# One row gather of a mixture-of-experts stage: 32 leftover rows packed, high part and low part, into one zero-padded block of 128

## The chip, the cores and the metric

The kernel runs on one core of one Trainium2 chip. The metric is the device time of one execution in microseconds (us). The kernel before was timed three times: the median is 1857.46 us, the lowest 1855.92 us and the highest 1864.35 us. A separate execution was profiled; the trace and every row below come from that one.

The core has five engines that run side by side and meet only at semaphores: TensorE (PE in the profile; its weight loads are shown apart, as PEld), VectorE (DVE), ScalarE (ACT), GpSimd (POOL) and SyncE (SP), which here only issues loads and stores.

## The reference

The reference is one inference step of a two-layer decoder over 256 prompt rows and 32 sample rows (8 sequences of 4) of width 1024. Layer 0 is block-sparse attention and a dense feed-forward; layer 1 is dilated window attention and a mixture of 8 experts, of which each row takes 2. Only the last part is touched by the change:

```
logits = x @ w_router                       # (288, 8)
top_val, top_idx = top_k(logits, 2)
gates = softmax(top_val)
# every expert e takes the rows that chose it, in blocks of 128 slots:
out[block] = swiglu(x_pad[toks], w_gu[e], w_down[e])
y[row] = sum over its two experts of gate * out[its slot]
```

All of it is float32.

## The kernel before

**Precision by parts.** TensorE gets 32-bit operands rounded to a shorter format ("fp32r"). To keep float32 accuracy every matrix is cut into a high part (the rounded value) and a low part (what the rounding left), and a product is three matmuls: high·high, high·low and low·high. The function `three` does this for the weights (lines 241, 242 and 243, the lines that fill the profile).

**Weights.** Weights arrive in pieces of 128 x 2048 floats (1 MB). SP loads them into a ring of six buffers `raw`; ACT makes the high part `whi` (L233), DVE the low part `wlo` (L237), each into a ring of three; PE uses a piece in 12 matmuls. ACT may start on piece p when PE is done with piece p-3 (semaphore `pieces_used`), SP may load piece p when DVE is done with piece p-6 (`pieces_split`). An expert has 42 pieces: 28 of gate and up weights, then 14 of down weights.

**Rows.** The 288 normalized rows lie in SBUF as three blocks (`TB`): 128, 128 and 32 rows, one row in a partition, 1024 columns. `hth` holds their high part, `htl` their low part. An expert's block of 128 slots is gathered by matmuls: `pm` is a one-hot matrix (row of the block by slot), written by DVE from a row's slot number (`one_hot`), and pm · rows, summed over the three blocks and both parts, gives the gathered rows in PSUM, in two halves of 512 columns (`gather`, L735). So a gather is 2 halves x 2 parts x 3 blocks = 12 matmuls; the third block is a matmul with 32 rows of weights. ACT copies each half to `xgs` (L1013), PE turns it in eight transposes (`gather_turn`, L745), ACT and DVE cut the result into `xgh` and `xgl`.

**Order in an expert.** The order on each engine is written out by hand, in the functions `expert(n)`. On PE the gate and up matmuls go in seven groups of four pieces. Between them stand: the transposes of the activations (`turn`, L755), the scatter of the expert before (`scatter`, L719: six matmuls twice), after piece 15 the turn of the one-hot matrix (`one_hot_turn`, L726: three transposes, released by DVE's last `add_rows`), and after piece 21 the gather for the next expert. DVE builds the next one-hot after piece 20's low part (L1426, at step 18 of its loop). Eight experts ran in this execution, so there are nine gathers, one ahead of the loop and eight in it, and eight one-hot turns.

**Ahead of the loop.** DVE, ACT and POOL make the rows: DVE copies them from PSUM (L1360), ACT squares them for the norm (L999), DVE scales (L1365), ACT makes `hth` (L1005), POOL makes `htl` (L400), DVE works out the routing in a long chain of small operations (L1383 to L1419), clears `pmt` (L1453), and writes the first one-hot. Then comes the first gather, and after it a second chain of small operations on DVE (L1465 to L1486) that stands ahead of the third piece's low part.

Of the kernel before, what the change touches and what calls it, by code (L numbers as in the profile page):

```python
# [22 lines left out]
F32 = mybir.dt.float32  # L23
F32R = mybir.dt.float32r
I32 = mybir.dt.int32
ALU = mybir.AluOpType
# [4 lines left out]
P = 128  # L31
D = 1024
# [3 lines left out]
NSAMP = NSEQ * QLEN  # L36
# [14 lines left out]
TB = [(0, P), (P, P), (2 * P, NSAMP)]  # L51
# [23 lines left out]
def build_program(nc, io):  # L75
    ctx = ExitStack()
    with ctx:
# [5 lines left out]
        def sem(name):  # L83
            if name not in named:
                named[name] = ctx.enter_context(nc.semaphore(name))
            return named[name]
# [11 lines left out]
        def at(name, off, shape, dt=F32):  # L98
            size = 4
            for s in shape[1:]:  # L100
                size *= s
            assert off + size <= REGION, name
            return nc.alloc_sbuf_tensor_at(name, shape, dt, offset=base + off)

        def con(name, rows=P):
            a, b = CONST[name]
            return cst[0:rows, a:b]
# [55 lines left out]

        xtok = at("xtok", 0, [P, 3, D])
        hth = at("hth", 12288, [P, 3, D], F32R)
        htl = at("htl", 24576, [P, 3, D], F32R)
        htok = at("htok", 36864, [P, 3, D])
        acth = at("acth", 36864, [P, KE, P], F32R)
        actl = at("actl", 51200, [P, KE, P], F32R)
# [6 lines left out]
        pm = at("pm", 86016, [P, 3, P], F32R)  # L176
# [8 lines left out]
        pcur = at("pcur", 95168, [P, 3])  # L185
# [9 lines left out]
        ps = [psum[:, i, :] for i in range(8)]  # L195
# [136 lines left out]
        @block.gpsimd  # L332
        def _(eng):
            eng.dma_start(pgt[0:1, :], io["page_table"]).then_inc(sem("pages_loaded"), 16)
            eng.wait_ge(sem("pages_loaded"), 16)

            def store(b, key, val):

                eng.wait_ge(sem(f"ktok_done_{b['tag']}"), b["nj"])
                eng.wait_ge(sem(f"vtok_done_{b['tag']}"), b["nj"])  # L340
                for buf, out in ((b["ktok"], key), (b["vtok"], val)):
                    eng.dma_start(out[0:SEQ, :].rearrange("(b p) n -> p b n", p=P), buf[:, 0:2, :]).then_inc(sem(f"kv_stored_{b['tag']}"), 16)
                    eng.dma_start(out[SEQ:T, :], buf[0:NSAMP, 2, :]).then_inc(sem(f"kv_stored_{b['tag']}"), 16)

            def caches(b, q, kt, vt):
                if q < NSEQ:
                    if q >= b["nk"]:

                        eng.wait_ge(sem(f"ktr_done_{b['tag']}"), (q - b["nk"] + 1) * b["kr"])
                    kt(q)  # L350

                if q >= 3:

                    eng.wait_ge(sem(f"spv_done_{b['tag']}"), q - 2)
                if q >= 1:
                    vt(q - 1)

            def paged(src, buf, q, done):
                for j in range(2):
                    pg = eng.value_load(pgt[0:1, 2 * q + j:2 * q + j + 1], min_val=0, max_val=NPHYS - 1)  # L360
                    eng.dma_start(buf[:, j, :], src[0][bass.ds(pg, 1), :, :].rearrange("a p n -> p (a n)")).then_inc(done, 16)

            def keys_a(q):
                paged(io["cache_a_k"], A["kraw"][:, 0], q, sem("kraw_loaded_a0"))

            def vals_a(q):
                if q == 0:

                    eng.wait_ge(sem("kv_stored_a"), 64)
                paged(io["cache_a_v"], A["vraw"][:, q % 2], q, sem(f"vraw_loaded_a{q % 2}"))  # L370

            caches(A, 0, keys_a, vals_a)
            store(A, io["ak"], io["av"])
            for q in range(1, NSEQ + 1):
                caches(A, q, keys_a, vals_a)

            def window(src, buf, q, done):
                eng.dma_start(buf, src[q].rearrange("(j p) n -> p j n", p=P)).then_inc(done, 16)

            def keys_b(q):  # L380
                window(io["cache_b_k"], B["kraw"][:, q % 2], q, sem(f"kraw_loaded_b{q % 2}"))

            def vals_b(q):
                window(io["cache_b_v"], B["vraw"][:, q % 2], q, sem(f"vraw_loaded_b{q % 2}"))


            eng.wait_ge(sem("added_dn"), KD)
            eng.dma_start(B["mask"][:, :], io["mask_b"]).then_inc(sem("mask_loaded_b"), 16)
            eng.wait_ge(sem("ktok_done_b"), B["nj"])
            eng.wait_ge(sem("vtok_done_b"), B["nj"])  # L390
            caches(B, 0, keys_b, vals_b)
            store(B, io["bk"], io["bv"])
            for q in range(1, NSEQ + 1):
                caches(B, q, keys_b, vals_b)
            eng.wait_ge(sem("o_split_b"), 1)
            eng.dma_start(rw[:, :, :], io["w_router"][0].rearrange("(k p) e -> p k e", p=P)).then_inc(sem("router_loaded"), 16)
            eng.dma_start(grow[:, :], io["g_rows"]).then_inc(sem("router_loaded"), 16)
            for c, (t0, w) in enumerate(TB):
                eng.wait_ge(sem("rows_hi"), c + 1)
                nc.gpsimd.tensor_tensor(htl[0:w, c, :], htok[0:w, c, :], hth[0:w, c, :].bitcast(F32), ALU.subtract).then_inc(sem("rows_lo"), 1)  # L400
            for b in "ab":
                eng.wait_ge(sem(f"kv_stored_{b}"), 64)

# [2 lines left out]
        def _(eng):  # L406
# [231 lines left out]
            for i in range(GU_P // 2):  # L638
                for part in range(2):
# [4 lines left out]
                    for s in range(2):  # L644
                        bank = ps[4 * (i % 2) + 2 * part + s]
                        for k in range(KD):
                            if i == 0 and part == 0 and s == 0:
                                eng.wait_ge(sem("norm_lo_ready"), norm_count("norm_f", k))
                            c = (k * 2 + s) * P
                            ins = three(bank[:, 0:T], whi[:, pc % SPL, c:c + P], wlo[:, pc % SPL, c:c + P], hh[:, k], hl[:, k],  # L650
                                        k == 0, k == KD - 1)
                        ins.then_inc(tile_sem(tiles_gu, 4 * i + 2 * part + s), 1)
            for m in range(KD + 2):
                if m < KD:
                    for part in range(2):
# [8 lines left out]
                        for k in range(11):  # L664
                            kk = 11 * part + k
                            if m == 0:
                                eng.wait_ge(sem("act_lo"), kk + 1)
                            ins = three(ps[m % 4][:, 0:T], whi[:, pc % SPL, k * P:(k + 1) * P], wlo[:, pc % SPL, k * P:(k + 1) * P],
                                        gh[:, kk], gl[:, kk], kk == 0, kk == KF - 1)
# [11 lines left out]
            for c, (t0, w) in enumerate(TB):  # L681
                for half in range(2):
                    if n == 0:
                        eng.wait_ge(sem("added_wob"), KD)
                    for u in range(4):
                        ins = nc.tensor.transpose(ps[n][0:w, u * P:(u + 1) * P], xT[:, 4 * half + u, t0:t0 + w], con("ident"))
# [4 lines left out]
            for c, (t0, w) in enumerate(TB):  # L691
                for k in range(KD):
                    ins = nc.tensor.matmul(ps[6][0:w, 8 * c:8 * c + 8], xT[:, k, t0:t0 + w], rwg[:, k], start=k == 0, stop=k == KD - 1)
# [8 lines left out]
            for d in range(3):  # L702
                wd = TB[d][1]
                ins = nc.tensor.matmul(ps[7][:, 32:40], con("ones", wd), sel[0:wd, 0, 8 * d:8 * d + 8], start=d == 0, stop=d == 2)
# [18 lines left out]
            def one_hot_turn(n):  # L723
                eng.wait_ge(sem("y_added"), 6 * n + 6)
                for c, (t0, w) in enumerate(TB):
                    ins = nc.tensor.transpose(ps[7][:, c * P:c * P + w], pm[0:w, c, :].bitcast(F32), con("ident", w)[:, 0:w])  # L726
                ins.then_inc(sem("one_hot_turned"), 1)

            def gather(n):

                eng.wait_ge(sem("one_hot"), n + 1)
                for half in range(2):
                    for part, v in enumerate((hth, htl)):
                        for c, (t0, w) in enumerate(TB):
                            ins = nc.tensor.matmul(ps[5 + half][:, :], pm[0:w, c, :], v[0:w, c, 512 * half:512 * half + 512],  # L735
                                                   start=part == 0 and c == 0, stop=part == 1 and c == 2)
                    ins.then_inc(sem("rows_gathered"), 1)

            def gather_turn(n):
# [336 lines left out]
        def _(eng):  # L1076
# [12 lines left out]
            def chain(ins):  # L1089

                steps[0] += 1
                ins.then_inc(sem("vector_step"), 1)
                eng.wait_ge(sem("vector_step"), steps[0])

            V = nc.vector
# [255 lines left out]
            for k in range(KD):  # L1351
                ins = V.tensor_scalar(rwg[:, k], rw[:, k], cst[:, g1 + k:g1 + k + 1], None, ALU.mult)
            ins.then_inc(sem("router_scaled"), 1)
            chain(V.memset(mst[:, :, :], 1.0))
            V.memset(sel[:, :, :], 0.0).then_inc(sem("mst_ready"), 1)
            n = 0
            for c, (t0, w) in enumerate(TB):
# [63 lines left out]
            def one_hot(n):  # L1421

                V.tensor_copy(pcur[:, :], pslot[:, :, bass.ds(n, 1)].rearrange("p c o -> p (c o)")).then_inc(sem("places_copied"), 1)
                eng.wait_ge(sem("places_copied"), n + 1)
                for c, (t0, w) in enumerate(TB):
                    ins = V.tensor_scalar(pm[0:w, c, :], con("slots", w), pcur[0:w, c:c + 1], None, ALU.is_equal)  # L1426
                ins.then_inc(sem("one_hot"), 1)

            def gather_lo(n, half):
                eng.wait_ge(sem("gathered_hi"), 2 * n + half + 1)  # L1430
# [18 lines left out]
                    .then_inc(sem("y_added"), 1)  # L1449


            V.memset(gcur[:, :], 0.0).then_inc(sem("gates_copied"), 1)
            V.memset(pmt[:, :, :].bitcast(F32), 0.0).then_inc(sem("pmt_copied"), 1)  # L1453
            one_hot(0)
# [199 lines left out]
```

## Time and profile before

| | before |
|---|---|
| median of 3 runs | 1857.46 us |
| profiled execution, its own time | 1856.88 us |
| its span, first to last instruction | 1855.2 us |
| mean granted TensorE clock | 0.956 |
| PE / PEld / DVE / ACT / POOL busy | 95 / 78 / 73 / 56 / 2 % of the span |

The profiled execution's own time is 1.7 us above its span and 0.6 us under the median of the runs. In a row of the timeline the columns are: start in us, duration in us, engine, line, operation, out<-in with partitions x elements, count; in brackets the idle time of that engine before it and what ended it. Matmuls overlap, since one starts before the one before it has left the array; what a matmul costs is therefore read from the distance of two starts, or from the chain of waits, where a piece is charged only for the time that it adds. A granted clock of 1.00 is 2.4 GHz and one of 0.50 is 1.2 GHz.

### The profile page before, as it was taken

To read this page: it belongs to the slowest core of one execution; us is meant where nothing else is said; L and a number is where in the kernel's file an instruction comes from. 1 tells how busy PE (TensorE), PEld (TensorE's weight loads), DVE (VectorE), ACT (ScalarE), POOL (GpSimd) and SP (SyncE) were. 2 spreads that over 40 slices of the span, in tenths; PEclk is the share of its full clock that TensorE was granted. 3 is DMA by queue.
4 is the path that set the end of the run, shared out by engine and by line. 5 is a ranking of instruction groups with operands and counts; after the bars stand their busy time and mean duration, and the time that the engine had idled before them with its cause. 6 is when DMAs were issued, how large, how long until landed. Compare 5 with 4: busy or idle time off the path is not lost.

```text
span 1855.2 us, 24910 instructions
## 1 busy us (share of the span) xinstructions
PE 1770.2 (95%) x9114; PEld 1444.4 (78%) x9114; DVE 1357.5 (73%) x1721; ACT 1038.6 (56%) x1043; POOL 44.7 (2%) x67
## 2 busy tenths in 40 slices
PE   7998989999989898689999999999999999999998
PEld 5786779999977667567887887887877878878776
DVE  5764316665557676678888888897897888888987
ACT  4333324443343243256776776766776767767765
POOL 0002100000000110100000000000000000000000
PEclk9998869999999987679999999999999999999999
DMA  9335413543653331059898998998998998999985
GB/s 319 99 114 188 149 56 114 171 155 111 185 170 107 118 117 48 13 202 343 319 362 317 359 345 315 360 344 327 354 336 330 352 346 318 362 317 359 343 319 205
DMA packets 232981, 453.17 MB, mean 244 GB/s; under 512 B 7584, under 2 KB 79264, under 8 KB 232784
## 3 DMA queue, kind: packets, MB, share of 16 engines
q1 hardware_dynamic: 224656, 422.13, 65.1%
q0 software_dynamic: 8256, 30.12, 4.9%
q8 instruction: 43, 0.70, 0.1%
q14 instruction: 26, 0.21, 0.0%
HBM read 447.50 MB, written 4.72 MB: 244 GB/s over the span
## 4 chain that ended last, share of the span: by engine, by line
PE 90%; DVE 5%; ACT 2%; issue 1%; DMA 1%; POOLq 0%; DVEq 0%; SPq 0%; ACTq 0%
PE psum L241 24%; PE psum L243 24%; PE psum L242 24%; PE psum L578 2%; PE psum L517 2%; PE psum L735 2%; PE psum L719 1%; PE psum L755 1%; PE psum L534 1%; PE psum L464 1%; PE psum L456 1%; PE psum L448 1%; PE psum L559 1%; DVE wlo L237 1%; PE psum L480 1%
## 5 line engine op out<-in xcount | busy, mean ns | idle before, releaser
L237 DVE TENSOR_TENSOR wlo<-raw,whi 128x2048 fp32r<-128x2048 f32 (+1 forms) x404 | 911.5, 2261 | 233.6 <-ACT whi L233 233.5
L233 ACT ACTIVATE whi<-raw 128x2048 fp32r<-128x2048 f32 (+1 forms) x404 | 764.8, 1895 | 326.8 <-PE psum L243 326.7
L241 PE MATMUL psum<-whi,xgh 128*128 128x512 f32 x896 | 360.5, 402 | 7.8 <-DVE wlo L237 6.4
L243 PE MATMUL psum<-whi,xgl 128*128 128x512 f32 x896 | 356.2, 398 | 0.0
L242 PE MATMUL psum<-wlo,xgh 128*128 128x512 f32 x896 | 354.4, 396 | 0.0
L241 PE MATMUL psum<-hh,whi 128*128 128x288 f32 x800 | 246.1, 308 | 11.6 <-DVE hl L1276 9.1
L243 PE MATMUL psum<-hh,wlo 128*128 128x288 f32 x800 | 239.9, 300 | 0.0
L242 PE MATMUL psum<-hl,whi 128*128 128x288 f32 x800 | 239.1, 299 | 0.0
L241 PEld LDWEIGHTS psum<-whi,xgh 128*128 128x128 f32 x896 | 169.3, 189 | 48.9 <-DVE wlo L237 6.9
L243 PEld LDWEIGHTS psum<-whi,xgl 128*128 128x128 f32 x896 | 169.2, 189 | 41.5
L242 PEld LDWEIGHTS psum<-wlo,xgh 128*128 128x128 f32 x896 | 169.4, 189 | 39.5
L241 PE MATMUL psum<-whi,acth 128*128 128x512 f32 x448 | 177.9, 397 | 0.0
L242 PE MATMUL psum<-wlo,acth 128*128 128x512 f32 x448 | 177.5, 396 | 0.0
L243 PE MATMUL psum<-whi,actl 128*128 128x512 f32 x448 | 176.9, 395 | 0.0
L241 PEld LDWEIGHTS psum<-hh,whi 128*128 128x128 f32 x800 | 153.1, 191 | 25.8 <-issue 12.2
L242 PEld LDWEIGHTS psum<-hl,whi 128*128 128x128 f32 x800 | 153.4, 192 | 0.8
L243 PEld LDWEIGHTS psum<-hh,wlo 128*128 128x128 f32 x800 | 152.7, 191 | 0.0
L241 PEld LDWEIGHTS psum<-whi,acth 128*128 128x128 f32 x448 | 84.1, 188 | 20.2
L243 PEld LDWEIGHTS psum<-whi,actl 128*128 128x128 f32 x448 | 84.1, 188 | 20.1
L242 PEld LDWEIGHTS psum<-wlo,acth 128*128 128x128 f32 x448 | 84.2, 188 | 19.6
L1043 ACT ACTIVATE sg<-psum 128x512 f32<-128x512 f32 x56 | 33.6, 600 | 46.1 <-PE psum L243 46.0
L241 PE MATMUL psum<-gh,whi 128*128 128x288 f32 x176 | 53.2, 302 | 1.2 <-issue 1.2
(290 smaller groups left out, 1805.4 us busy)
## 6 DMA issues: line engine op xcount, KB each, us to landing
raw<-in_w_gu_moe SPq DMA_DIRECT2D x226, 1024.0 KB, 5.4
raw<-in_w_down_moe SPq DMA_DIRECT2D x112, 1024.0 KB, 5.3
raw<-in_w_gu_dense SPq DMA_DIRECT2D x22, 1024.0 KB, 5.0
raw<-in_w_qkv_a SPq DMA_DIRECT2D x12, 1024.0 KB, 12.3
raw<-in_w_down_dense SPq DMA_DIRECT2D x16, 704.0 KB, 4.6
kraw_a<-in_cache_a_k POOLq DMA_DIRECT2D x16, 512.0 KB, 4.8
vraw_a<-in_cache_a_v POOLq DMA_DIRECT2D x16, 512.0 KB, 4.9
raw<-in_w_q_b SPq DMA_DIRECT2D x6, 1024.0 KB, 5.0
```

The lines of the kernel that those rows point to most:

```text
L233: nc.scalar.activation(whi[:, p % SPL, 0:size], raw[:, p % RAW, 0:size], ACT.Copy).then_inc(hi_ready, 1)
L237: nc.vector.tensor_tensor(wlo[:, p % SPL, 0:size], raw[:, p % RAW, 0:size], whi[:, p % SPL, 0:size].bitcast(F32), ALU.subtract).then_inc(p ...
L241: nc.tensor.matmul(out, lh, rh, start=start, stop=False)
L242: nc.tensor.matmul(out, lh, rl, start=False, stop=False)
L243: return nc.tensor.matmul(out, ll, rh, start=False, stop=stop)
L448: nc.tensor.matmul(ps[4 + r // 4 % 2][0:8, 0:T], cst[:, c:c + 8], sq[:, r % 2], start=r % 4 == 0, stop=r % 4 == 3)\
L456: nc.tensor.matmul(ps[6][:, 0:T], con("rot"), sq[:, 2 + r % 2], start=True, stop=True)\
L464: nc.tensor.matmul(ps[7][:, 0:T], cst[0:8, c:c + P], rs[0:8, 1], start=True, stop=True)\
L517: ins = nc.tensor.matmul(ps[SS_BANK][0:rows, 0:T], b["qblk"][:, u % 2, j * rows:(j + 1) * rows], b["keys"][:, j, :], start=j == 0, stop=j ...
L578: ins = nc.tensor.matmul(out, b["vraw"][:, u % 2, c, j * P:(j + 1) * P], b["spt"][:, u % 2, c, 8 * j:8 * j + 8], start=c == 0, stop=c == 1)
L735: ins = nc.tensor.matmul(ps[5 + half][:, :], pm[0:w, c, :], v[0:w, c, 512 * half:512 * half + 512], start=part == 0 and c == 0, stop=part ...
L1043: nc.scalar.activation(sg[:, :], ps[0][:, :], ACT.Silu).then_inc(sem("silu_done"), 1)
```

## The change

The 32 rows of the third block get their high and their low part into one block of 128 partitions: partitions 0 to 31 of `hth[:, 2, :]` hold the high part as before, 32 to 63 the low part, 64 to 127 zeros. The one-hot matrix of the third block holds the same 32 rows twice, in partitions 0 to 31 and 32 to 63, and zeros below. One matmul over all 128 partitions then adds high and low part of the 32 rows. A half of a gather takes five matmuls of full 128 rows of weights in place of six, of which two had 32. The turn of the one-hot matrix works on three full blocks. Two clears of padding are added on DVE (64 x 1024 and 64 x 128), a fourth small one-hot operation in every `one_hot`, and a wait on POOL ahead of its third subtraction.

```diff
-        htl = at("htl", 24576, [P, 3, D], F32R)
+        htl = at("htl", 24576, [P, 2, D], F32R)
...
             for c, (t0, w) in enumerate(TB):
                 eng.wait_ge(sem("rows_hi"), c + 1)
-                nc.gpsimd.tensor_tensor(htl[0:w, c, :], htok[0:w, c, :], hth[0:w, c, :].bitcast(F32), ALU.subtract).then_inc(sem("rows_lo"), 1)
+                if c == 2:
+                    eng.wait_ge(sem("rows_lo"), 2)
+                low = htl[:, c, :] if c < 2 else hth[NSAMP:2 * NSAMP, 2, :]
+                nc.gpsimd.tensor_tensor(low, htok[0:w, c, :], hth[0:w, c, :].bitcast(F32), ALU.subtract).then_inc(sem("rows_lo"), 1)
...
                 for c, (t0, w) in enumerate(TB):
-                    ins = nc.tensor.transpose(ps[7][:, c * P:c * P + w], pm[0:w, c, :].bitcast(F32), con("ident", w)[:, 0:w])
+                    ins = nc.tensor.transpose(ps[7][:, c * P:(c + 1) * P], pm[:, c, :].bitcast(F32), con("ident"))
...
                 for half in range(2):
-                    for part, v in enumerate((hth, htl)):
-                        for c, (t0, w) in enumerate(TB):
-                            ins = nc.tensor.matmul(ps[5 + half][:, :], pm[0:w, c, :], v[0:w, c, 512 * half:512 * half + 512],
-                                                   start=part == 0 and c == 0, stop=part == 1 and c == 2)
+                    for i, (v, c) in enumerate(((hth, 0), (hth, 1), (htl, 0), (htl, 1), (hth, 2))):
+                        ins = nc.tensor.matmul(ps[5 + half][:, :], pm[:, c, :], v[:, c, 512 * half:512 * half + 512],
+                                               start=i == 0, stop=i == 4)
                     ins.then_inc(sem("rows_gathered"), 1)
...
             chain(V.memset(mst[:, :, :], 1.0))
+            V.memset(hth[64:P, 2, :].bitcast(F32), 0.0)
             V.memset(sel[:, :, :], 0.0).then_inc(sem("mst_ready"), 1)
...
                 for c, (t0, w) in enumerate(TB):
-                    ins = V.tensor_scalar(pm[0:w, c, :], con("slots", w), pcur[0:w, c:c + 1], None, ALU.is_equal)
-                ins.then_inc(sem("one_hot"), 1)
+                    V.tensor_scalar(pm[0:w, c, :], con("slots", w), pcur[0:w, c:c + 1], None, ALU.is_equal)
+                V.tensor_scalar(pm[NSAMP:2 * NSAMP, 2, :], con("slots", NSAMP), pcur[0:NSAMP, 2:3], None, ALU.is_equal).then_inc(sem("one_hot"), 1)
...
+            V.memset(pm[64:P, 2, :].bitcast(F32), 0.0)
             V.memset(gcur[:, :], 0.0).then_inc(sem("gates_copied"), 1)
```

On PE, at the gather inside an expert, the program stood like this before (`am` is the activations being turned, `pm` the one-hot, `xgh` and `xgl` the gathered rows of the current expert; lines are those of the kernel before):

```order
L243 MATMUL psum<-whi,xgl 128x512
L755 MATMUL psum<-cst,am 128x128 x4
L731 REGISTER_ALU
L735 MATMUL psum<-hth,pm 128x512 x3
L735 MATMUL psum<-htl,pm 128x512 x3
L735 MATMUL psum<-hth,pm 128x512 x3
L735 MATMUL psum<-htl,pm 128x512 x3
L410 REGISTER_ALU
L241 MATMUL psum<-whi,xgh 128x512
```

and stands like this now (the last of the first half and the first two of the second are printed together as three):

```order
L757 MATMUL psum<-cst,am 128x128 x4
L734 REGISTER_ALU
L737 MATMUL psum<-hth,pm 128x512 x2
L737 MATMUL psum<-htl,pm 128x512 x2
L737 MATMUL psum<-hth,pm 128x512 x3
L737 MATMUL psum<-htl,pm 128x512 x2
L737 MATMUL psum<-hth,pm 128x512
```

Twelve matmuls became ten; what stands around them did not move.

On DVE, between the routing and the first gather, the program stood like this before (`pslot` and `gslot` are the slots and gates of all rows, `pmt` is the turned one-hot, `pcur` the slots of the expert at hand):

```order
L1418 COPY pslot<-sel 128x3x8 [waits vector_step]
L1419 COPY gslot<-sel 128x3x8 [waits vector_step]
L1452 MEMSET gcur 128x3 [waits vector_step]
L1453 MEMSET pmt 128x384
L1423 COPY pcur<-pslot 128x3
L1426 TENSOR_SCALAR pm<-cst,pcur 128x128 [waits places_copied]
L1426 TENSOR_SCALAR pm<-cst,pcur 128x128
L1426 TENSOR_SCALAR pm<-cst,pcur 32x128
L237 TENSOR_TENSOR wlo<-raw,whi 128x2048 [waits hi_ready] x2
```

and stands like this now:

```order
L1422 COPY gslot<-sel 128x3x8 [waits vector_step]
L1455 MEMSET pm 64x128 [waits vector_step]
L1456 MEMSET gcur 128x3
L1457 MEMSET pmt 128x384
L1426 COPY pcur<-pslot 128x3
L1429 TENSOR_SCALAR pm<-cst,pcur 128x128 [waits places_copied]
L1429 TENSOR_SCALAR pm<-cst,pcur 128x128
L1429 TENSOR_SCALAR pm<-cst,pcur 32x128
L1430 TENSOR_SCALAR pm<-cst,pcur 32x128
L237 TENSOR_TENSOR wlo<-raw,whi 128x2048 [waits hi_ready] x2
```

One clear and one small operation more stand ahead of the first gather; the operation of L1430 is there in every expert too, ahead of a `wlo`.

## Rows read from the trace of the kernel before

**Rows 1.** The page: the busy time of each engine, and the chain that ended last.
```profile
PE 1770.2 (95%) x9114; PEld 1444.4 (78%) x9114; DVE 1357.5 (73%) x1721; ACT 1038.6 (56%) x1043; POOL 44.7 (2%) x67
PE 90%; DVE 5%; ACT 2%; issue 1%; DMA 1%; POOLq 0%; DVEq 0%; SPq 0%; ACTq 0%
```

**Rows 2.** Windows, gather to gather: length, busy us by engine, clock, DMA share, GB/s.
```profile
874.26:1003.74 129.48, 129.48 (x569) 102.61 (x568) 110.28 (x72) 93.03 (x66) 0.00 (x0) 1.00 0.95 341
1651.14:1780.62 129.48, 129.48 (x569) 102.61 (x568) 110.29 (x72) 93.00 (x66) 0.00 (x0) 1.00 0.96 341
```

**Rows 3.** Waits, 811 to 1845 us: engine line <- releaser: us, times, longest.
```profile
ACT whi L233 <- PE psum L243: 253.6, 257, 8.0
DVE wlo L237 <- ACT whi L233: 153.5, 199, 4.2
```

**Rows 4.** Timeline around the gather in the loop's first expert.
```profile
873.66 0.60 PE L755 MATMUL psum<-cst,am 128*128 128x128 f32 x4
874.02 1.13 PE L735 MATMUL psum<-hth,pm 128*128 128x512 f32 x3
874.66 0.18 PEld L735 LDWEIGHTS psum<-hth,pm 32*128 32x128 f32 x1 [0.36 <-issue]
875.08 0.30 PEld L735 LDWEIGHTS psum<-htl,pm 128*128 128x128 f32 x2 [0.24 <-issue]
...
878.33 0.50 PE L241 MATMUL psum<-whi,xgh 128*128 128x512 f32 x1
878.67 0.40 PE L242 MATMUL psum<-wlo,xgh 128*128 128x512 f32 x1
```

**Rows 5.** Chain of waits in the loop: start, us added, what.
```profile
818.08 1.39 PE psum L719 x6
...
874.26 4.14 PE psum L735 x12
```

**Rows 6.** Timeline: an activation turn at 849 us, then the one-hot turn at 855 us.
```profile
849.58 0.60 PE L755 MATMUL psum<-cst,am 128*128 128x128 f32 x4
850.26 0.40 PE L242 MATMUL psum<-wlo,xgh 128*128 128x512 f32 x1
...
854.99 0.73 DVE L1448 SCALAR_TENSOR_TENSOR xtok<-psum,gcur,xtok 32x512 f32<-32x512 f32 x1
855.78 0.61 PE L726 MATMUL psum<-cst,pm 128*128 128x128 f32 x3
856.15 0.13 PEld L726 LDWEIGHTS psum<-cst,pm 32*128 32x128 f32 x1 [0.17 <-issue]
856.66 0.39 PE L242 MATMUL psum<-wlo,xgh 128*128 128x512 f32 x1
```

**Rows 7.** Timeline of the first gather, ahead of the loop, and two matmuls behind it.
```profile
785.08 1.91 PE L735 MATMUL psum<-hth,pm 128*128 128x512 f32 x3 [3.04 <-DVE pm L1426]
792.54 1.97 PE L745 MATMUL psum<-cst,xgs 128*128 128x128 f32 x8
798.65 0.63 PE L241 MATMUL psum<-whi,xgh 128*128 128x512 f32 x1
799.07 0.63 PE L242 MATMUL psum<-wlo,xgh 128*128 128x512 f32 x1
810.41 0.79 PE L241 MATMUL psum<-whi,xgh 128*128 128x512 f32 x1 [6.42 <-DVE wlo L237]
```

**Rows 8.** Chain of waits from 754 to 800 us, ahead of the first gather.
```profile
758.40 0.30 DVE sel L1355
758.70 3.53 DVE xtok L1360 x6
...
783.83 0.38 DVE pmt L1453
784.26 0.68 DVE pm L1426 x3
```

**Rows 9.** Timeline from 767 to 776 us: POOL's three subtractions, DVE's routing beside them.
```profile
767.78 8.01 POOL L400 TENSOR_TENSOR htl<-htok,hth 128x1024 fp32r<-128x1024 f32 x3 [24.82 <-ACT hth L1005]
773.57 2.27 DVE L1387 TENSOR_TENSOR sel<-sel,cst 128x24 f32<-128x24 f32 x1
```

**Rows 10.** Line 226, the loads, from 820 to 1840 us: issue to landing.
```profile
DMA to landing us min/median/max: 4.7/5.4/8.6
```

## The prediction, made before the changed kernel ran

> **What bounds the kernel now.** I read the page first. TensorE is busy 95% of the span and holds 90% of the chain that ended last [rows 1]. A share of busy time is a mean over stages, so I next cut the expert loop into windows from one gather to the next. Every expert takes 129.48 us, and PE is busy in all of it, at the full clock, with DVE at 110 us and ACT at 93 us [rows 2]. The list of waits says who runs behind whom: ACT waited 257 times for PE and DVE 199 times for ACT [rows 3], and PE waited for a `wlo` only once, at 810.41 us where the loop starts [rows 7]. So inside the loop time follows PE's issue of matmuls one for one, and ACT and DVE follow PE. Then I looked at the timeline of the two places that the change touches on PE, and at the chain of waits ahead of the loop, where DVE and not PE sets the pace.
>
> **The gather in the loop.** Three matmuls starting at 874.02 us are followed by the next three, whose weights load at 875.08 us: 1.06 us for three [rows 4]. A plain stream goes much faster: six L719 matmuls of the same shape and weights add 1.39 us, 0.232 us each [rows 5], so three should take 0.70. The difference sits at the matmul with 32 rows of weights. Its load begins after PEld stood idle for 0.36 us, and the load of the full block behind it after 0.24 us more [rows 4]. In a plain stream loads are pulled ahead under the running matmul. I read this as an array that must empty when the number of weight rows changes, on the way in and on the way out. The whole gather adds 4.14 us [rows 5]. The way out is also paid by the L241 matmul behind it: it starts at 878.33 and its successor at 878.67, 0.34 us instead of 0.23 [rows 4]. From the first gather matmul to that L242 it is 878.67 - 874.02 = 4.65 us.
>
> After the change these are ten full matmuls and the one L241, all with 128 rows of weights: 11 x 0.232 = 2.55 us. Saved: 4.65 - 2.55 = 2.10 us per gather. Of these, two matmuls fewer are 0.46 us, and the switching that goes is the other 1.64. Eight gathers lie in the loop: 16.8 us. Bounds: a full gather matmul can hardly beat 0.232. From above, the nearest row is the mean of today's gather, 4.14 / 12 = 0.345; with that, ten cost 3.45, the L241 keeps its 0.34, and a gather saves 4.65 - 3.79 = 0.86 us, 6.9 in all. I take 0.232, because L719 is the same shape with the same kind of operands.
>
> A rule of the Trainium skill speaks against this size: "TensorE: Matmul & The Clock Gate", section "Why this matters for your kernels", says that a lone matmul with 32 weight rows takes as long as one with 128. By that only the two dropped matmuls would count. The page "TensorEngine Tiling (Array Packing)", section "Key Properties", says that a change of tiling mode drains the engine. The spacing in the timeline goes with the second.
>
> **The one-hot turn.** The three transposes start at 855.78 us, directly behind DVE's last add (854.99 + 0.73 = 855.72), and the second matmul behind them starts at 856.66: 0.88 us. Here too the 32-row load stands idle before it, 0.17 us. The activation turn of four full transposes goes from 849.58 to the second matmul behind it at 850.26 in 0.68 us [rows 6]. One transpose less is 0.09 us (four take 874.02 - 873.66 = 0.36 in rows 4), so three full ones should take 0.59. Saved 0.29 us, times 8: 2.3 us. The release by DVE stays. If the switch cost stayed and the third transpose, now 128 wide instead of 32, cost a further 0.09, the turns would lose 0.7 us in all. I take the gain.
>
> **The first gather.** It runs at the half clock. It starts at 785.08 us and the transposes behind it at 792.54: 7.46 us [rows 7]. Matmuls at this clock start 0.42 to 0.43 us apart (798.65, 799.07), so ten take 4.27. Saved: 3.19 us. It is on the path: `xgl` follows it, then DVE's chain of small operations, then the `wlo` for which PE waits 6.42 us, to 810.41 [rows 7]. Everything in this line moves up with the gather. Should the denser stream bring the full clock sooner, PE would still wait for DVE at 810 us; only the piece between gather and `xgl` could gain, under 2 us.
>
> **What is added.** (1) The clear of 64 x 1024 of `hth` stands on DVE between two clears and the copies L1360. Clears cost about 1 ns per element of a partition: `sel`, 288 elements, 0.30 us, and `pmt`, 384, 0.38 us [rows 8]. So 1024 cost 1.05 us. The chain of waits runs through `sel` straight into the six copies, and through ACT and DVE to the first gather, so I charge all of it: 1.05 us. Between nothing (if something else hid it) and 1.1. (2) The clear of 64 x 128 of `pm`: 0.13 us, on the same path. (3) The fourth one-hot operation: 0.68 / 3 = 0.22 us [rows 8], on the path once, ahead of the first gather. In the loop it comes ahead of a `wlo` on DVE, which waits for ACT 199 times [rows 3]. DVE's 110.3 us become 110.5 of then 127.1: hidden. If that cover were gone it would cost 8 x 0.22 = 1.8 us. (4) POOL's third subtraction waits for its own two before it. POOL works until 767.78 + 8.01 = 775.79 and DVE's small operations crawl beside it, the one at 773.57 taking 2.27 us and ending at 775.84, with POOL [rows 9]. POOL is thus on the path here. The wait opens a gap of a tenth or two, in which DVE also gets an operation in; writing 32 partitions lower should not change POOL's time. I take 0, and bound it by one such operation, 2.3 us, either way. Added in all: 1.40 us.
>
> **Who could be late next.** ACT and DVE now lose 2.1 us of waiting per expert; DVE has 129.48 - 110.28 = 19.2 us of it. The loads: 341 GB/s over an expert of 129.48 us become 341 x 129.48 / 127.1 = 347. A load lands 4.7 to 8.6 us after its issue [rows 10]. Between the end of piece p-6's `wlo` and the start of piece p's `whi` lie about six pieces of 12 x 0.232 = 2.8 us, less some 4 us for splitting: 12 us. The margin over 8.6 is larger than the 2.1 us that the gather stops giving.
>
> **The sum.** 16.8 + 2.3 + 3.2 - 1.4 = 20.9 us. The profiled execution took 1856.88 us (span 1855.2), which gives 1836.0. The median of the runs lies 0.6 above that execution, so 1836.6; I say 1836.5, or 1.1% faster.
>
> **Rivals.**
> A. The empty time does not come from the 32 rows but from alternating operands, and each gather matmul keeps its 0.345 us. Then the loop gathers save 8 x 2 x 0.345 = 5.5 us, the turns nothing, the first gather 2 x 7.46 / 12 = 1.2 less the added 1.4: 5.3 in all, 1852. For it: no row of before shows a gather without 32-row blocks. Against it: the idle stands exactly at the 32-row load and at the one behind it, and L719 alternates between `oh` and `ol` at full pace.
> B. The skill's rule above holds literally, and 32 rows cost what 128 do: 8 x 0.46 = 3.7 us and the first gather 2 x 0.427 = 0.9 less the added 1.4, about 3.2 us in all, 1854. Against it are the same rows.
> C. The loads are at their limit. An expert then keeps the 129.48 us that 341 GB/s allow, and PE, which was never idle, waits 2.4 us per expert. If the wait falls in one piece, the clock drops as it did behind the 6.42 us wait of rows 7, where matmuls then took 0.43 us for almost 4 us, 1.9 us lost. Eight times that is 15 us, less 1.8 for the prologue: 1870, slower. It decides once sustained load falls under 347 GB/s. For it: a DMA share of 0.95 [rows 2]. Against it: no wait of ACT for a load, and landings within 8.6 us.
> D. It does what it says but in the prologue POOL or the clear costs 2 us more: 1839, inside my range.
>
> **How the numbers follow.** Forecast (with D) 90%, A 4%, B 3%, C 3%. The measurement of this kernel can tell about 0.5% (9 us) from no change. Faster: 90 and a little of A, 0.91; same 0.07; slower 0.02. The range: the unknown costs give -2.3 to +2.3 for POOL, up to 2 us for the clock ahead of the loop, 3 us for the turns and the hidden operation, and medians of three scatter upwards (1855.9 to 1864.4). I take 1832 to 1842.
>
> **What would show it.** In the profile of the changed kernel: windows of gather to gather of 127.1 us; ten gather matmuls adding 2.3 us; the L241 behind them 0.23 us ahead of its L242; no idle PEld inside the gather; the one-hot turn 0.6 us to the second matmul; the first gather 4.3 us; the `hth` clear 1.05 us between `mst` and the copies; PE still never waiting for a `wlo` after 811 us. The prediction is wrong if gather matmuls still start 0.3 us or more apart, or if ACT waits for loads.

## The result, and the profile after

The changed kernel takes 1839.33 us, the median of 6 runs (1833.36 to 1841.81), against 1858.65 us (1852.26 to 1864.35) for the kernel before, 6 runs. The ratio is 0.9889, 95% interval 0.9861 to 0.9917: 1.1% faster. A second comparison on another occasion gave 0.9887 (0.9869 to 0.9905). The forecast was 1836.5 us in a range of 1832 to 1842.

The span of the profiled execution went from 1855.2 to 1838.3 us, 16.9 less. The page and the windows from gather to gather answer to [rows 1, 2]:

```profile
PE 1751.9 (95%) x9096; PEld 1443.0 (78%) x9096; DVE 1361.8 (74%) x1732; ACT 1038.8 (57%) x1043; POOL 44.9 (2%) x67
...
PE 90%; DVE 5%; ACT 2%; issue 1%; DMA 1%; DVEq 0%; POOLq 0%; SPq 0%; ACTq 0%
```

```profile
874.53:1001.94 127.41, 127.41 (x566) 102.44 (x566) 110.69 (x73) 93.03 (x66) 0.00 (x0) 1.00 0.97 346
1639.00:1766.40 127.40, 127.40 (x566) 102.44 (x566) 110.67 (x73) 93.03 (x66) 0.00 (x0) 1.00 0.97 346
```

An expert takes 127.41 us instead of 129.48, within 0.01 us in every one of the seven windows. The shares on the page hardly moved: a kernel that its PE bounds looks the same after PE got less to do. The timeline of the gather answers to [rows 4]:

```profile
874.29 0.71 PE L737 MATMUL psum<-hth,pm 128*128 128x512 f32 x2
874.60 0.42 PEld L737 LDWEIGHTS psum<-htl,pm 128*128 128x128 f32 x2
874.84 0.63 PE L737 MATMUL psum<-htl,pm 128*128 128x512 f32 x2
...
876.69 0.40 PE L241 MATMUL psum<-whi,xgh 128*128 128x512 f32 x1
876.92 0.40 PE L242 MATMUL psum<-wlo,xgh 128*128 128x512 f32 x1
```

From the first gather matmul to the L242 behind it now lie 2.63 us instead of 4.65. No weight load stands idle, and L242 follows L241 by 0.23 us instead of 0.34. The one-hot turn answers to [rows 6]:

```profile
856.09 0.55 PE L729 MATMUL psum<-cst,pm 128*128 128x128 f32 x3
856.71 0.39 PE L242 MATMUL psum<-wlo,xgh 128*128 128x512 f32 x1
```

0.62 us instead of 0.88. Both together save 2.28 us per expert, but an expert is only 2.07 us shorter. The rest is a new wait. The chain of waits in the loop shows it as a piece that no row of before has, 3.5 us ahead of the gather:

```profile
856.09 0.55 PE psum L729 x3
...
871.08 0.45 PE psum L241
...
874.53 2.32 PE psum L737 x10
```

The timeline there says what released it:

```profile
867.69 0.67 DVE L1429 TENSOR_SCALAR pm<-cst,pcur 128x128 fp32r<-128x128 f32 x3
868.37 0.28 DVE L1430 TENSOR_SCALAR pm<-cst,pcur 32x128 fp32r<-32x128 f32 x1
868.68 2.29 DVE L237 TENSOR_TENSOR wlo<-raw,whi 128x2048 fp32r<-128x2048 f32 x1
871.03 0.19 PEld L241 LDWEIGHTS psum<-whi,xgh 128*128 128x128 f32 x1 [0.39 <-DVE wlo L237]
871.36 0.40 PE L242 MATMUL psum<-wlo,xgh 128*128 128x512 f32 x1
```

And the same place in the kernel before:

```profile
867.63 0.67 DVE L1426 TENSOR_SCALAR pm<-cst,pcur 128x128 fp32r<-128x128 f32 x3
868.22 2.27 DVE L237 TENSOR_TENSOR wlo<-raw,whi 128x2048 fp32r<-128x2048 f32 x1
870.63 0.19 PEld L241 LDWEIGHTS psum<-whi,xgh 128*128 128x128 f32 x1
870.86 0.40 PE L241 MATMUL psum<-whi,xgh 128*128 128x512 f32 x1
```

Before, the low part of the next piece began 0.59 us after the one-hot, was ready at 870.49, the weight load of its first matmul started at 870.63, under the matmul before, and that matmul at 870.86. Now it begins 0.99 us after the one-hot (868.68 - 867.69) and is ready at 870.97. The load comes at 871.03, and its matmul starts with it, about 0.1 us late; the next matmul follows 0.33 us behind it instead of 0.23, which is the other 0.1. Together they add 0.45 us to the chain where a neighbour adds 0.23.

Ahead of the loop the chain of waits answers to [rows 8] and [rows 7]:

```profile
761.43 0.91 DVE hth L1357
762.45 0.30 DVE sel L1358
762.75 3.52 DVE xtok L1363 x6
...
787.54 0.17 DVE pm L1455
787.84 0.38 DVE pmt L1457
788.28 0.67 DVE pm L1429 x3
788.96 0.29 DVE pm L1430
...
789.38 4.55 PE psum L737 x10
```

From the router scaling on DVE (757.09 before, 759.97 after) to the first gather matmul it is 29.41 us instead of 27.99. From there to the L241 that waits for the third piece's low part (810.41 before, 811.17 after) it is 21.79 instead of 25.33.

The 16.9 us by stage:

| stage | before | after | saved |
|---|---|---|---|
| start to the router scaling | 757.09 | 759.97 | -2.88 |
| router scaling to first gather | 27.99 | 29.41 | -1.42 |
| first gather to the late L241 | 25.33 | 21.79 | 3.54 |
| from there to the loop's first gather | 63.85 | 63.36 | 0.49 |
| seven experts, gather to gather | 906.36 | 891.87 | 14.49 |
| last gather to the end | 74.58 | 71.90 | 2.68 |

The first row is not the change's: no line there changed. Over the profiles taken for this study that point fell between 750.2 us and 761.0 us, while an expert repeats within 0.03 us in each of them. The spread is about as large as that of the whole times (1852.26 to 1864.35 us for the kernel before). The experiments are therefore read by two numbers that leave it out: the time of an expert, and the time from the first router scaling to the end of the span (1098.1 us before, 1078.3 after). Experiments 1 to 5 ran once each; their whole times, in the order below, are 1852.39, 1846.51, 1838.92, 1841.51 and 1860.61 us, against one run of the kernel before of 1853.36 (1860.30 beside the fifth).

### The profile page after: what moved, and what is told of

It reads as the page before. It is cut to its first block, busy times and chain, and to the rows that moved or that the text cites. A ratio compares the mean times of both kernels' runs of the same rounds, so it can differ in the third digit from the quotient of the medians.

```text
span 1838.3 us, 24886 instructions
## 1 busy us (share of the span) xinstructions
PE 1751.9 (95%) x9096; PEld 1443.0 (78%) x9096; DVE 1361.8 (74%) x1732; ACT 1038.8 (57%) x1043; POOL 44.9 (2%) x67
## 4 chain that ended last, share of the span: by engine, by line
PE 90%; DVE 5%; ACT 2%; issue 1%; DMA 1%; DVEq 0%; POOLq 0%; SPq 0%; ACTq 0%
PE psum L241 24%; PE psum L242 24%; PE psum L243 24%; PE psum L581 3%; PE psum L520 3%; PE psum L722 1%; PE psum L757 1%; PE psum L737 1%; PE psum L467 1%; PE psum L537 1%; PE psum L459 1%; PE psum L451 1%; PE psum L562 1%; DVE wlo L237 1%; PE psum L483 1%
## 5 line engine op out<-in xcount | busy, mean ns | idle before, releaser
L237 DVE TENSOR_TENSOR wlo<-raw,whi 128x2048 fp32r<-128x2048 f32 (+1 forms) x404 | 911.8, 2262 | 213.5 <-ACT whi L233 213.1
L241 PE MATMUL psum<-whi,xgh 128*128 128x512 f32 x896 | 359.5, 401 | 8.5 <-DVE wlo L237 7.1
L242 PE MATMUL psum<-wlo,xgh 128*128 128x512 f32 x896 | 354.6, 396 | 0.0
L241 PE MATMUL psum<-hh,whi 128*128 128x288 f32 x800 | 246.2, 308 | 11.7 <-DVE hl L1278 9.1
L242 PE MATMUL psum<-hl,whi 128*128 128x288 f32 x800 | 239.6, 300 | 0.0
L241 PEld LDWEIGHTS psum<-whi,xgh 128*128 128x128 f32 x896 | 169.1, 189 | 50.7 <-DVE wlo L237 10.6
L242 PEld LDWEIGHTS psum<-wlo,xgh 128*128 128x128 f32 x896 | 169.2, 189 | 39.1
L241 PE MATMUL psum<-whi,acth 128*128 128x512 f32 x448 | 178.3, 398 | 0.0
L242 PE MATMUL psum<-wlo,acth 128*128 128x512 f32 x448 | 177.9, 397 | 0.0
L241 PEld LDWEIGHTS psum<-hh,whi 128*128 128x128 f32 x800 | 154.1, 193 | 25.9 <-issue 12.2
L242 PEld LDWEIGHTS psum<-hl,whi 128*128 128x128 f32 x800 | 153.2, 191 | 0.8
L241 PEld LDWEIGHTS psum<-whi,acth 128*128 128x128 f32 x448 | 84.1, 188 | 20.4
L242 PEld LDWEIGHTS psum<-wlo,acth 128*128 128x128 f32 x448 | 84.2, 188 | 19.0
L241 PE MATMUL psum<-gh,whi 128*128 128x288 f32 x176 | 53.2, 302 | 1.2 <-issue 1.2
```

What stands on the lines that cost most here:

```text
L237: nc.vector.tensor_tensor(wlo[:, p % SPL, 0:size], raw[:, p % RAW, 0:size], whi[:, p % SPL, 0:size].bitcast(F32), ALU.subtract).then_inc(p ...
L241: nc.tensor.matmul(out, lh, rh, start=start, stop=False)
L242: nc.tensor.matmul(out, lh, rl, start=False, stop=False)
```

## The experiments

The gather length below is always from the first gather matmul to the L242 behind the gather, in the loop's second expert.

### 1. The 32-row matmuls side by side

```diff
-                    for part, v in enumerate((hth, htl)):
-                        for c, (t0, w) in enumerate(TB):
+                    for i, (v, c) in enumerate(((hth, 0), (hth, 1), (htl, 0), (htl, 1), (hth, 2), (htl, 2))):
+                        w = TB[c][1]
```

> The kernel before with one edit: in each half of a gather the two matmuls with 32 rows of weights stand next to each other, at the end (hth 0, hth 1, htl 0, htl 1, hth 2, htl 2). Still 12 matmuls. Measured by the distance from the first gather matmul to the L242 behind the gather (4.65 us before, 2.63 us in the changed kernel). Theory (the array empties when the number of weight rows changes, about 0.41 us for one visit to 32 rows): 13 x 0.232 + 2 visits x 0.41 = 3.8 us, an expert 0.8 us shorter than 129.48, so 128.7. Rival 1 (a 32-row matmul is slow in itself, whatever stands beside it): 13 x 0.232 + 4 x 0.41 = 4.7 us, an expert 129.5. Rival 2 (all gather matmuls are slow at 0.345 us because operands alternate): 4.6 us, 129.5.

Measured: 3.86 us, an expert 128.69 us. Nothing was taken away, twelve matmuls with four of 32 rows as before, and 0.8 us went. The timeline of one half and of the start of the next:

```profile
1004.99 0.62 PE L735 MATMUL psum<-htl,pm 128*128 128x512 f32 x2
1005.54 0.18 PEld L735 LDWEIGHTS psum<-hth,pm 32*128 32x128 f32 x1 [0.36 <-issue]
1005.54 0.49 PE L735 MATMUL psum<-hth,pm 32*128 32x512 f32 x1
1005.65 0.18 PEld L735 LDWEIGHTS psum<-htl,pm 32*128 32x128 f32 x1
1005.88 0.39 PE L735 MATMUL psum<-htl,pm 32*128 32x512 f32 x1
1006.20 0.30 PEld L735 LDWEIGHTS psum<-hth,pm 128*128 128x128 f32 x2 [0.37 <-issue]
```

The first 32-row load stands idle, the second does not, the full block behind them does again. Two small matmuls in one visit cost the same surcharge as one did alone (experiment 2 gives 0.40 us for either). The price is on the change of the row count, not on the small matmul. Both rivals fall.

### 2. Twelve full matmuls

```diff
-  ins = nc.tensor.matmul(ps[5 + half][:, :], pm[0:w, c, :], v[0:w, c, 512 * half:512 * half + 512],
+  ins = nc.tensor.matmul(ps[5 + half][:, :], pm[:, c, :], v[:, c, 512 * half:512 * half + 512],
...
+            V.memset(hth[:, 2, :].bitcast(F32), 0.0)
+            V.memset(htl[:, 2, :].bitcast(F32), 0.0)
...
+            chain(V.memset(pm[:, 2, :].bitcast(F32), 0.0))
```

> The kernel before with its third block padded by zeros to 128 rows in hth, htl and the one-hot, so that a gather is 12 matmuls of full 128 rows; nothing is packed, the one-hot turn keeps its 32-row transpose. It separates the count of matmuls from the number of weight rows. Theory (switching): 13 x 0.232 = 3.0 to 3.1 us from the first gather matmul to the L242 behind, an expert 129.48 - 1.6 = 127.9 us, so that packing to ten is worth only the last 0.46 us. Rival (the skill's rule, 32 rows cost what 128 do): 4.65 us and 129.5, as before. Rival (0.345 us each): 4.4 us. Ahead of the loop two clears of 1024 and one of 128 are added, some 2 us.

Measured: 3.07 us, an expert 127.90 us. The chain charges the twelve with 2.75 us, 0.229 each. Padding alone gives back 1.59 of the 2.04 us per gather; packing twelve into ten gives the other 0.45. Ahead of the loop the clears cost 2.4 us (30.40 from router scaling to first gather, 27.99 before; some 2 expected). A visit, that is going to fewer weight rows and back, costs (4.66 - 3.07) / 4 = 0.40 us with one 32-row matmul in it (the kernel before) and (3.86 - 3.07) / 2 = 0.40 us with two (experiment 1).

The rule of the Trainium skill that the prediction quotes ("TensorE: Matmul & The Clock Gate", section "Why this matters for your kernels"), that a lone matmul with 32 weight rows takes as long as one with 128, agrees with this for the second 32-row matmul of a visit, which adds no more than a full one. It is short by 0.40 us for a 32-row matmul that stands between full ones.

### 3. The packed block without padding

```diff
-  ins = nc.tensor.transpose(ps[7][:, c * P:(c + 1) * P], pm[:, c, :].bitcast(F32), con("ident"))
+  ins = nc.tensor.transpose(ps[7][:, c * P:c * P + w], pm[0:w, c, :].bitcast(F32), con("ident", w)[:, 0:w])
...
+  h = P if c < 2 else 2 * NSAMP
-  ins = nc.tensor.matmul(ps[5 + half][:, :], pm[:, c, :], v[:, c, 512 * half:512 * half + 512],
+  ins = nc.tensor.matmul(ps[5 + half][:, :], pm[0:h, c, :], v[0:h, c, 512 * half:512 * half + 512],
...
-            V.memset(hth[64:P, 2, :].bitcast(F32), 0.0)
...
-            V.memset(pm[64:P, 2, :].bitcast(F32), 0.0)
```

> The changed kernel without the padding: high and low part of the 32 rows packed into 64 partitions, the fifth matmul of each half with 64 rows of weights; both clears of padding go, and the one-hot turn has its 32-row transpose back. Theory (any change of the row count empties the array): 11 x 0.232 + 2 x 0.41 = 3.4 us from the first gather matmul to the L242 behind, and the turn back from 0.62 to 0.88 us; an expert 127.41 + 0.8 + 0.26 = 128.4 us. Rival (only 32-row matmuls are slow, 64 are as good as 128, and padding is for nothing): 2.63 us, an expert 127.7 us. Ahead of the loop the clears give back about 1.3 us.

Measured: 3.40 us, an expert 128.44 us. A visit to 64 rows costs (3.40 - 2.62) / 2 = 0.39 us, the same as one to 32. The one-hot turn takes 0.88 us again, and from the router scaling to the first gather it is 28.02 us instead of 29.41, so the missing clears give back 1.4. So the padding is not decoration: without it an expert keeps only half of the gain (129.48 - 128.44 = 1.04 of 2.07 us).

```profile
994.91 0.18 PEld L738 LDWEIGHTS psum<-hth,pm 64*128 64x128 f32 x1 [0.36 <-issue]
...
995.34 0.30 PEld L738 LDWEIGHTS psum<-hth,pm 128*128 128x128 f32 x2 [0.24 <-issue]
```

Its single whole time, 1838.92 us, reads as good as the changed kernel's. That is the stage ahead: this execution came to the router scaling at 750.2 us, ten ahead of the others. From there to the end it took 1087.0 us, 8.7 more than the changed kernel.

### 4. A fifth small operation on DVE

```diff
+        spare = at("spare", 32768, [P, P], F32R)
...
+  V.tensor_scalar(spare[0:NSAMP, :], con("slots", NSAMP), pcur[0:NSAMP, 2:3], None, ALU.is_equal)
   V.tensor_scalar(pm[NSAMP:2 * NSAMP, 2, :], con("slots", NSAMP), pcur[0:NSAMP, 2:3], None, ALU.is_equal).then_inc(sem("one_hot"), 1)
```

> The changed kernel with one more small one-hot operation (32 x 128) on DVE in every expert, written to an unused tile. In the changed kernel the L241 behind piece 20 waits for its low part, 0.22 us in every expert, which the kernel before did not show. Theory (the fourth one-hot operation made DVE late there, and the slack is used up): a fifth adds its whole 0.3 to 0.4 us to that wait; an expert takes 127.7 to 127.8 us instead of 127.41. Rival (the wait comes from the shorter gather or from the loads): the wait stays 0.22 us and an expert 127.4 us.

Measured: an expert 127.59 us, 0.18 more, and the load behind piece 20 stands idle 0.6 us instead of 0.4. (One line more stands ahead, so L241 and L237 are L242 and L238 here.)

```profile
PEld psum L242 <- DVE wlo L238: 4.6, 8, 0.6
```

The mechanism holds, the size is under what I expected. The operation moved the low part by 0.20 us (1.19 us behind the one-hot's start instead of 0.99), and 0.18 of it came through to the expert.

### 5. The fourth operation alone, in the kernel before

```diff
-                ins.then_inc(sem("one_hot"), 1)
+                V.tensor_scalar(pm[NSAMP:2 * NSAMP, 2, :], con("slots", NSAMP), pcur[0:NSAMP, 2:3], None, ALU.is_equal).then_inc(sem("one_hot"), 1)
```

> The kernel before with one part of the change alone: the fourth one-hot operation on DVE (to partitions 32 to 63, which nobody reads there). In the kernel before the low part of piece 21 was ready at 870.49 us and its first matmul started at 870.86; in the changed kernel the operation put the low part 0.4 us later, and the matmul 0.2 us late. Theory: the same here, an expert takes 129.48 + 0.2 = 129.7 us with a wait for a low part at the L241 behind piece 20. Rival (the wait needs the shorter gather, which gives DVE less time to catch up): 129.48 us and no such wait.

Measured: an expert 129.68 us, 0.20 more than before, with the wait at the same matmul:

```profile
870.05 0.67 DVE L1426 TENSOR_SCALAR pm<-cst,pcur 128x128 fp32r<-128x128 f32 x3
870.73 0.28 DVE L1427 TENSOR_SCALAR pm<-cst,pcur 32x128 fp32r<-32x128 f32 x1
871.04 2.29 DVE L237 TENSOR_TENSOR wlo<-raw,whi 128x2048 fp32r<-128x2048 f32 x1
873.38 0.19 PEld L241 LDWEIGHTS psum<-whi,xgh 128*128 128x128 f32 x1 [0.38 <-DVE wlo L237]
```

So the shorter gather has no part in it. The operation puts the low part 0.40 us later, half of that is absorbed, PE waits the other half.

### 6. Three operations again, the clear on POOL, and the changed kernel beside it

```diff
+            eng.wait_ge(sem("kv_stored_b"), 64)
+            nc.gpsimd.memset(hth[64:P, 2, :].bitcast(F32), 0.0).then_inc(sem("pad_cleared"), 1)
+            eng.wait_ge(sem("pad_cleared"), 1)
...
-            V.memset(hth[64:P, 2, :].bitcast(F32), 0.0)
...
             chain(V.tensor_scalar(s3(10), s3(10), -1.0, None, ALU.add))
+            chain(V.tensor_copy(sel[NSAMP:2 * NSAMP, 10, 16:24], sel[0:NSAMP, 10, 16:24]))
...
-                for c, (t0, w) in enumerate(TB):
-                    V.tensor_scalar(pm[0:w, c, :], con("slots", w), pcur[0:w, c:c + 1], None, ALU.is_equal)
-                V.tensor_scalar(pm[NSAMP:2 * NSAMP, 2, :], con("slots", NSAMP), pcur[0:NSAMP, 2:3], None, ALU.is_equal).then_inc(sem("one_hot"), 1)
+                for c in range(3):
+                    ins = V.tensor_scalar(pm[:, c, :], con("slots"), pcur[:, c:c + 1], None, ALU.is_equal)
+                ins.then_inc(sem("one_hot"), 1)
...
-            V.memset(pm[64:P, 2, :].bitcast(F32), 0.0)
```

> The changed kernel with its DVE work taken back: the slots of the 32 rows are copied once to partitions 32 to 63, so that the one-hot of the third block is one operation over 128 partitions (three in all, as before; the padding of the one-hot needs no clear), and the clear of 64 x 1024 goes to POOL, which is idle there. Theory (the 0.22 us wait behind piece 20 is the fourth operation's, and the clear lies on the path): an expert 127.41 - 0.22 = 127.2 us, eight times 1.8 us; from the router scaling to the first gather matmul 29.4 - 1.2 (clear) - 0.2 - 0.3 + 0.2 = 27.9 us; about 3.2 us less in all, near 1836 us. Rival (wait from elsewhere): 127.4 us an expert and only the 1.5 us ahead of the loop. A difference this small may not be told from run-to-run scatter of the whole; the trace tells it by stage.

> The changed kernel once more, beside the one above on the same chip. All theories: 0.989 of the kernel before, an expert 127.4 us; the time up to the router scaling moves by some us from run to run, as no line there changed.

Measured for the new version: an expert 127.20 us, PE waiting for no low part in the loop, and 27.9 us from the router scaling to the first gather: both as expected. From the router scaling to the end it takes 1076.1 us, against 1078.1 of the changed kernel profiled beside it (an expert 127.39). The whole times do not tell them apart: 1836.47 us (ratio to before 0.9886, interval 0.9868 to 0.9904) and 1836.48 us (0.9887, 0.9869 to 0.9905). The 2 us are seen by stage only, one execution of each; that the version is faster in the whole is not shown. They are also less than the 3.2 expected: 1.5 come ahead of the loop and 1.4 from the seven experts, as expected, and 0.8 are lost again between the first gather and the loop's first gather and behind the last gather (granted clock 0.62 from first gather to first L241, where the changed kernel beside it has 0.71).

## Why the prediction was right

The time fell as forecast, by the mechanism forecast. Its steps, one by one:

- **Gather in the loop.** Forecast 2.10 us each, measured 4.65 - 2.63 = 2.02. The split was forecast as 0.46 for the count and 1.64 for switching; experiment 2 gives 0.45 and 1.59. That it is the change of the row count rests on experiments 1 and 3. "The array empties" remains my reading of the idle weight loads; the runs show where the time lies and its size, not what the array does in it.
- **One-hot turn.** Forecast 0.29, measured 0.88 - 0.62 = 0.26. DVE's add still releases it.
- **First gather.** Forecast 3.19. The transposes behind it start 4.37 us after it instead of 7.46, which is 3.09. From there to the first L241 it is 2.93 us instead of 3.38, and I put these 0.45 us down to the clock (last section). PE still waits for DVE behind it, now 7.07 us.
- **Added ahead of the loop.** Forecast 1.40, measured 1.42; the match is partly luck, since each part came out larger and the gap at POOL, put at nothing, gave some back. The `hth` clear cost 1.17 (0.91 of work, which is what the two clears of [rows 8] give by their difference, 0.83 ns for each further element; the rest is idle time between the clears), the `pm` clear 0.22, the fourth operation 0.29. The gap that POOL's new wait opens gave 0.25 back: DVE's routing got two small operations through in it.
- **The fourth operation in the loop: the step that failed.** I called it hidden, since DVE has 19 us of idle time in an expert, and the sign "PE still never waiting for a `wlo` after 811 us" did not come: its weight load waits in each of the eight experts. The cost is 0.2 us per expert, 1.7 us in all, in experiments 5 and 6 by adding and by removing it. That the prediction priced a lost cover at 1.8 us, near the 1.7, is luck: it took the operation at 0.22 us and all of it as lost, but the operation moves the low part by 0.40 us and half of that is lost. The idle time of DVE lies elsewhere. Here the low part of the next piece stands right behind the one-hot. From its end to the start of its first matmul it was 870.86 - 870.49 = 0.37 us, but the weight load of that matmul already stood at 870.63, 0.14 us behind the low part. By the matmul alone 0.40 us would have been all but covered, but the load comes too late to run under the matmul before, and PE lost 0.2. The prediction subtracted neither.
- **Loads.** Not late: ACT waits for none in the list of waits of the loop, with 346 GB/s in an expert, and landing takes 4.7 to 7.9 us, no more than before. Rival C did not happen.

```profile
DMA to landing us min/median/max: 4.7/5.1/7.9
```

The sum was 20.9; from the router scaling to the end it is 1098.1 - 1078.3 = 19.8. The miss of 1.1 is 1.7 for the fourth operation, 0.9 for slightly smaller savings in gather and turn and 0.1 for the first gather, less some 1.5 that came at the ends of the loop: 0.45 behind the first gather, 0.45 between the late L241 and the loop's first gather, where PE worked 3.0 us at the half clock instead of 4.0, and 0.66 behind the last gather, where the mean granted clock was 0.98 instead of 0.95. The sum had no term for these 1.5 us, so they are luck; without them the sum would have missed by 2.6. The profiled whole moved 16.9 because the stages ahead were 2.9 longer in that execution. On the medians it is 19.3.

Rival A (0.345 us a matmul) falls with experiment 2, where twelve full ones with alternating operands cost 0.229. Its price in the prediction is not consistent: at the same 0.345 us a gather saves 0.86 us in the bound and 0.69 in the rival, because the bound sets 4.65 us of the timeline against shares of the chain, which is 0.17 shorter. Rival B falls with experiments 1 and 2, and D with the 1.42 above.

## What to carry to other kernels

In a stream of full matmuls, look for the lone one with fewer weight rows: at the full clock it costs a surcharge of 0.40 us here, with 32 rows and with 64, which the idle time of the weight load shows. Put the odd ones side by side, or pad them to full height and use the padding to pack a second product in. And when work is added to an engine with much idle time, do not set it against the engine's total: look at that very place, and subtract the end of what follows it from the start of what waits for that, the weight load and not only the matmul.

## What the hardware showed that I had not expected

**The clock behind the first gather.** The first gather starts at the half clock. In the kernel before PE worked from 785.08 to past 794 us with little pause, and the granted clock stayed at 0.50. So it did in the other two versions with 32-row matmuls in the gather, experiments 1 and 5. In all six executions without them it rose within the stretch from gather to the first L241, to a mean between 0.62 and 0.77. Windows of that stretch for before, experiment 1 and experiment 5:

```profile
785.08:795.92 10.84, 9.43 (x21) 4.63 (x21) 5.69 (x5) 3.15 (x5) 0.00 (x0) 0.50 0.56 193
787.30:796.90 9.60, 8.25 (x20) 4.81 (x20) 5.63 (x5) 3.09 (x5) 0.00 (x0) 0.50 0.61 215
787.55:798.40 10.85, 9.43 (x20) 4.64 (x21) 5.82 (x5) 3.15 (x5) 0.00 (x0) 0.50 0.55 193
```

And for after, experiment 2 and experiment 3:

```profile
789.38:796.68 7.30, 5.63 (x19) 4.12 (x19) 5.82 (x5) 3.04 (x5) 0.00 (x0) 0.70 0.51 178
790.31:797.61 7.30, 5.64 (x20) 4.23 (x21) 5.69 (x5) 3.04 (x5) 0.00 (x0) 0.77 0.53 178
778.26:786.15 7.89, 6.37 (x19) 3.61 (x19) 5.82 (x5) 3.14 (x5) 0.00 (x0) 0.71 0.55 186
```

Experiment 3 also changes the row count in every half, between 128 and 64, and its clock rose all the same. So changing the row count does not by itself keep the clock low. Why the three versions with 32-row matmuls stayed at 0.50 is open: these are nine executions, and no run varies only the moment at which the gather falls. The higher clock was worth 0.45 us here, because PE then waits for DVE.

**The scatter sits ahead of the router scaling.** That point moved between 750.2 and 761.0 us. The code up to there is the same in all executions but the one at 761.0, the new version of experiment 6, which has its clear on POOL there; the changed kernel beside it reached the point at 760.1. Between 660 and 750 us the granted clock was 0.83 before, 0.79 after, and 0.85 in experiment 3, which reached it first. That fits a clock that rises and falls in the attention stages at other moments each time; no run here isolates it.
